# Attention on pairs of heads, with the softmax scale applied by the matrix product that transposes the probabilities

## The chip, the cores and the metric

The kernel runs on one core of one Trainium2 chip. The metric is the device time of one launch in microseconds (us), lower is better. The engines are TensorE (PE; its weight loads are listed apart as PEld), VectorE (DVE), ScalarE (ACT), GpSimd (POOL) and SyncE (SP).

## What is computed

Two transformer-like blocks in float32 on 512 tokens of width 1024. The first (four mixers, gates and a feed-forward layer) is not touched. The second has two layers. In each, 12 heads of 64 columns attend among the tokens and 4 heads read 256 memory rows; a projection and a convolutional feed-forward layer follow.

```python
# layer 0: causal attention with a forget term
c = lax.cumsum(log_f, axis=2)                  # per head, log_f = log_sigmoid(...)
sc = einsum(q, k) * dh ** -0.5
sc = sc + ci[..., :, None] - c[..., None, :]
sc = where(kpos <= qpos, sc, NEG)
out = softmax(sc) @ v
# layer 1: q, k with rotary embedding; three dilated branches of the same
# scores, which the kernel joins to one softmax with an additive 512x512 mask
# both layers, memory heads, no mask
sc = einsum(qm, km) * HEAD_DIM ** -0.5
out = softmax(sc) @ vm
h = h + merge_heads(heads) @ w_out[layer]
```

The term `ci` is the same along a row of scores and drops out of the softmax, so the kernel adds only the part that depends on the key.

## The kernel before, in words

Weights stream in as 334 pieces of 128 x 1024. Each weight product is done as three products of fp32r operands (high x high, high x low, low x high; `product`, L1277): the activations stand split in `h_hi`/`h_lo` (for projections from x) and `g_hi`/`g_lo` (for projections from hidden values or heads). POOL issues the loads of the weights and makes their low parts (L320 to L328).

Five engines run programs of their own, in the order in which their code is written, and wait for each other by semaphores. There is no scheduler: a wait in an engine's code holds everything behind it on that engine. Around attention the stages of a layer are:

1. Projections from x: 6 tiles of q (128 columns, so two heads each), 6 of k, 6 of v, in layer 0 one for the forget gates, 2 for the queries of the memory heads. DVE takes them out of the PSUM banks. In layer 0 it writes q and k at L628, one instruction per head into rows 0 to 63 of the tiles `q` and `k` of the arena: a head has all its 64 columns on rows 0 to 63 and a 512-column stretch of its own. In layer 1 ACT copies first (L1192), PE makes the rotated copy (`swap`, L1315) and DVE adds up (L638 to L641). v is transposed by PE (`turn_values`, L1328) and put back by DVE (L650).
2. Before the first of these DVE sets row 64 of all of `q` to 1.0 (L622, a memset of 1 x 8192), in both layers. In layer 0 the running sum of the forget gates is copied by one SP DMA into row 64 of `k`, so that a score product over 65 rows adds the forget term.
3. Memory keys and values: four more tiles from `mn`, the normalised memory.
4. Attention (`attention` on PE and the loops over `UNITS` on DVE and ACT): 64 units per layer, one unit is a head and a block of 128 queries. A unit of a mixing head has 128, 256, 384 or 512 keys, of a memory head 256. Per unit:
   - PE: the scores into bank ps0 to ps3 in turn (L1345); in layer 0 a second product adds the causal mask to the last 128 columns: identity x mask, both f32 (L1348).
   - DVE: in layer 1 the mask is added (L697); then the row maximum (L699).
   - ACT: exponential with the row sum (L1217) into one of 4 buffers `probs`.
   - DVE: reciprocal (L705), the whole row of probabilities times it (L706).
   - PE: one transpose per 128 keys into bank ps4 or ps5 (L1375), which ACT copies to `pt` (L1225).
   - After the first unit of the next head PE multiplies the values by `pt` (L1361, 4 products of 512, 384, 256 and 128 columns) into rows 0 to 63 or 64 to 127 of bank ps6 or ps7; ACT and DVE split the result into `g_hi` and `g_lo` (L1209, L686, 64 rows each).

   PE's loop writes the scores of unit u+2 ahead of the transposes of unit u:

```python
for u, (head, qb, width, _) in enumerate(UNITS):
    if u + 2 < len(UNITS):
        scores(u + 2)                       # from u = 4 waits for exped of u-4
    pe.wait_ge(S("probs"), before + u + 1)
    if u >= 2:
        pe.wait_ge(S("probs_kept"), before + u - 1)
    ...                                     # transposes of unit u
    if qb == 0 and head:
        head_output(head - 1)
```

   ACT's loop does the exponential of unit s, then the copy of unit s-2. DVE's loop does the maximum of unit s, then the scaling of unit s-1.
5. Projection of the heads into x (8 tiles) and the feed-forward layer.

The mask of layer 0 (640 KB, `mask_fox`) is loaded by SP into `work` after the forget row has landed. That of layer 1 is loaded in the same way after its rotary step.

## Time and profile before

| what | value |
| --- | --- |
| runs | 2654.08 us median of 3 (2653.63 to 2654.12) |
| profiled execution | 2655.1 us, span 2653.3 us |
| mean granted TensorE clock | 0.915 |
| PE busy | 2316.0 us, 87% of the span |
| DVE, ACT, POOL busy | 1475.5, 450.8, 845.2 us (56%, 17%, 32%) |
| chain that ended last, by engine | PE 71%, DVE 19%, DMA 5%, ACT 2%, issue 2% |
| attention of layer 0 | 1292.0 to 1434.9 us of the span |
| attention of layer 1 | 2022.0 to 2209.0 us of the span |

How to read it. Times count from the start of the span. An engine is busy while an instruction of it runs; matmuls are pipelined, so the duration listed for one holds its passage through the array too, and the step from the start of one to the start of the next tells what it costs in a row of them. A row of the timeline joins like instructions: `x8` is eight matmul records, and a product of f32 operands has two records (two passes) where a transpose or a product of fp32r operands has one. `[0.44 <-ACT arena L1225]` is idle time of the engine ahead of the row, and what ended it. The granted clock is 1.00 at 2.4 GHz and 0.50 at 1.2 GHz; between two such levels a mean over a stretch tells how it was divided. Row labels in the trace name the tile written and the tiles read.

### The profile page before, as it was taken

To read this page: it belongs to the slowest core of one execution; us is meant where nothing else is said; L and a number is where in the kernel's file an instruction comes from. 1 tells how busy PE (TensorE), PEld (TensorE's weight loads), DVE (VectorE), ACT (ScalarE), POOL (GpSimd) and SP (SyncE) were. 2 spreads that over 40 slices of the span, in tenths; PEclk is the share of its full clock that TensorE was granted. 3 is DMA by queue.
4 is the path that set the end of the run, shared out by engine and by line. 5 is a ranking of instruction groups with operands and counts; after the bars stand their busy time and mean duration, and the time that the engine had idled before them with its cause. 6 is when DMAs were issued, how large, how long until landed. Compare 5 with 4: busy or idle time off the path is not lost.

```text
span 2653.3 us, 26772 instructions
## 1 busy us (share of the span) xinstructions
PE 2316.0 (87%) x10172; PEld 1774.1 (67%) x10172; DVE 1475.5 (56%) x2162; ACT 450.8 (17%) x887; POOL 845.2 (32%) x1006
## 2 busy tenths in 40 slices
PE   1967999669669999989888999998988889999995
PEld 1745677557548888868655878787765336878784
DVE  6368866744674422574454654636654554736464
ACT  1010002111000000210354211112102442201011
POOL 1312333101224444434201444444332003444442
PEclk9978999756879999999899999999997678999998
DMA  7635687312869999968503889898774006889895
GB/s 238 145 70 110 125 166 161 76 30 51 261 188 230 193 195 193 193 147 182 114 1 80 190 180 193 174 194 187 167 154 101 1 1 128 190 184 193 179 195 130
DMA packets 114935, 390.73 MB, mean 147 GB/s; under 512 B 20460, under 2 KB 20972, under 8 KB 114296
## 3 DMA queue, kind: packets, MB, share of 16 engines
q0 software_dynamic: 96192, 350.27, 62.0%
q1 hardware_dynamic: 18616, 38.76, 4.2%
q8 instruction: 81, 1.33, 0.2%
q14 instruction: 46, 0.38, 0.1%
HBM read 386.33 MB, written 2.62 MB: 147 GB/s over the span
## 4 chain that ended last, share of the span: by engine, by line
PE 71%; DVE 19%; DMA 5%; issue 2%; ACT 2%; POOL 0%; SPq 0%; DVEq 0%; ACTq 0%
PE ps L1277 57%; PE ps L1361 4%; DMA arena<-in_ada 3%; PE ps L1345 2%; DMA w_lo<-in_w 2%; DVE small L699 1%; DVE arena L437 1%; PE ps L1375 1%; DVE work L706 1%; PE ps L1497 1%; DVE work L542 1%; DVE h_lo L354 1%; DVE g_lo L686 1%; DVE arena L725 1%; DVE g_lo L354 1%
## 5 line engine op out<-in xcount | busy, mean ns | idle before, releaser
L1277 PE MATMUL ps<-h_hi,w_hi 128*128 128x512 f32 x1760 | 713.2, 405 | 50.2 <-DVE h_lo L354 28.3
L320 POOL DMA_DIRECT2D w_hi<-in_w x334 | 186.1, 557 | 1623.6 <-PE ps L1277 1622.7
L1277 PE MATMUL ps<-h_lo,w_hi 128*128 128x512 f32 x1760 | 695.0, 395 | 0.0
L1277 PE MATMUL ps<-h_hi,w_lo 128*128 128x512 f32 x1760 | 694.2, 394 | 0.0
L1277 PEld LDWEIGHTS ps<-h_hi,w_hi 128*128 128x128 f32 x1760 | 336.7, 191 | 143.0 <-issue 36.1
L1277 PE MATMUL ps<-g_hi,w_hi 128*128 128x512 f32 (+1 forms) x880 | 346.6, 394 | 54.5 <-DVE g_lo L354 21.2
L1277 PEld LDWEIGHTS ps<-h_lo,w_hi 128*128 128x128 f32 x1760 | 337.2, 192 | 74.0 <-issue 6.7
L1277 PEld LDWEIGHTS ps<-h_hi,w_lo 128*128 128x128 f32 x1760 | 336.4, 191 | 71.9
L325 POOL TENSOR_SCALAR w_lo<-w_hi 128x1024 fp32r<-128x1024 f32 x334 | 359.5, 1076 | 36.5 <-DMA w_hi<-in_w 30.7
L1277 PE MATMUL ps<-g_lo,w_hi 128*128 128x512 f32 (+1 forms) x880 | 341.6, 388 | 0.0
L1277 PE MATMUL ps<-g_hi,w_lo 128*128 128x512 f32 (+1 forms) x880 | 341.3, 388 | 0.0
L328 POOL DMA_DIRECT2D w_lo<-in_w x334 | 300.3, 899 | 116.3 <-POOL w_lo L325 116.3
L1277 PEld LDWEIGHTS ps<-g_hi,w_hi 128*128 128x128 f32 x880 | 169.6, 193 | 99.4 <-DVE g_lo L354 23.7
L1277 PEld LDWEIGHTS ps<-g_lo,w_hi 128*128 128x128 f32 x880 | 170.2, 193 | 32.6 <-issue 0.7
L1277 PEld LDWEIGHTS ps<-g_hi,w_lo 128*128 128x128 f32 x880 | 169.5, 193 | 33.6
L1243 ACT ACTIVATE arena<-arena,vec 128x512 f32<-128x512 f32 x88 | 71.8, 816 | 416.4 <-DVE arena L720 408.9
L731 DVE TENSOR_TENSOR x<-ps,x 128x512 f32<-128x512 f32 x48 | 33.2, 692 | 186.5 <-PE ps L1277 186.5
L720 DVE TENSOR_TENSOR arena<-ps,work 128x512 f32<-128x512 f32 x88 | 60.8, 691 | 98.8 <-PE ps L1277 97.3
L1345 PE MATMUL ps<-arena 64*128 64x256 f32 (+7 forms) x256 | 113.7, 531 | 1.2 <-DVE work L677 1.2
L725 DVE SCALAR_TENSOR_TENSOR arena<-arena,vec 128x511 f32<-128x511 f32 x88 | 111.7, 1270 | 3.6 <-ACT arena L1243 0.6
L952 DVE TENSOR_TENSOR arena<-arena 128x512 f32<-128x512 f32 x32 | 53.0, 1657 | 76.9 <-ACT arena L1170 76.9
L353 DVE CAST g_hi<-arena 128x512 fp32r<-128x512 f32 (+1 forms) x100 | 82.8, 828 | 6.3 <-ACT arena L1104 2.9
(335 smaller groups left out, 2246.3 us busy)
## 6 DMA issues: line engine op xcount, KB each, us to landing
w_hi<-in_w POOLq DMA_DIRECT2D x334, 512.0 KB, 3.8
w_lo<-in_w POOLq DMA_DIRECT2D x334, 512.0 KB, 5.6
arena<-in_ada SPq DMA_DIRECT2D x48, 512.0 KB, 8.4
x<-in_xT SPq DMA_DIRECT2D x1, 2048.0 KB, 16.2
x<-in_xT SPq DMA_DIRECT2D x4, 512.0 KB, 4.9
arena<-in_memT SPq DMA_DIRECT2D x2, 1024.0 KB, 5.1
out_y<-arena SPq DMA_DIRECT2D x1, 2048.0 KB, 6.3
work<-in_mask_fox SPq DMA_DIRECT2D x1, 640.0 KB, 7.0
```

The source lines that it names most:

```text
L320: pool.dma_start(w_hi[:, q % SLOTS, :], A["w"][q]).then_inc(S(f"high_in{q % SLOTS}"), 16)
L325: pool.tensor_scalar(w_lo[:, q % SLOTS, :], w_hi[:, q % SLOTS, :].bitcast(F32), -1.0, 0.0, ALU.mult, ALU.add).then_inc(S("negated"), 1)
L328: pool.dma_start(w_lo[:, q % SLOTS, :], A["w"][q], accum_op=ALU.add).then_inc(S(f"low_in{q % SLOTS}"), 16)
L353: do(dve.tensor_copy(hi, src))
L354: do(dve.tensor_tensor(lo, src, hi.bitcast(F32), ALU.subtract), name)
L720: do(dve.tensor_tensor(cv_m["z"][:, side, :], tile()[:], rstd, ALU.mult), "conv_scaled")
L725: do(dve.scalar_tensor_tensor(dst[:, 1:], z[:, :T - 1], w(1), dst[:, 1:], ALU.mult, ALU.add))
L952: do(dve.tensor_tensor(s, r, r, ALU.mult), "relu_used")
L1243: do(act.activation(c[:, j % 2, :], cv_m["z"][:, side, :], ACT.Identity, scale=V("cw2", at), bias=V("cb2", 44 * layer + 22 * side + j0 + j ...
L1277: mm = pe.matmul(bank, w[:, slot, cols], a(k), start=(k == 0 and i == 0), stop=(k == blocks - 1 and i == 2))
L1345: mm = pe.matmul(ps[u % BANKS][:, 0:width], at_m["q"][0:rows, head, P * qb:P * qb + P], keys, start=True, stop=not masked)
L1361: mm = pe.matmul(ps[6 + head % 2][out_rows, q0:T], values, at_m["pt"][:, b, q0:T], start=(b == 0), stop=(b == blocks - 1))
```

## The change

It groups the heads in pairs, 8 per layer (6 mixing, 2 memory), so that there are 32 units per layer in place of 64.

- Layout: `q`, `k` and `km` hold a pair in one 512-column stretch, the even head on rows 0 to 63, the odd one on 64 to 127. The evictions at L628, L641, L668 and L672 become one instruction of 128 rows each in place of two of 64. The ones row and its memset (L622) go.
- Scores: two products of 64 rows, one per head, into two neighbouring banks (L1362).
- Forget term, layer 0: the running sum is split into three fp32r parts (4 small DVE instructions), which 6 SP DMAs put on rows 0 to 2 and 64 to 66 of `h_lo`. For each head an fp32r product with ones in three of 64 rows (`parts_r`) adds it to all columns (L1366).
- Causal mask, layer 0: fp32r product of `eye_r` and `causal_r` (L1368), both 128 x 128. With `parts_r` they are loaded at the program's start by three POOL DMAs, which stand ahead of the first `load_low`. The 640 KB load of `mask_fox` is gone.
- Softmax: one DVE maximum for both heads (L706), in layer 1 one mask addition for both; two exponentials (L1233); one reciprocal of two columns (L712); DVE then writes for each head the 128 x 128 identity times the reciprocal (L716) and leaves the probabilities as they are.
- Transpose: a plain f32 product of each block of probabilities with that diagonal matrix (L1397).
- Outputs: for each key block one product per head, into rows 0 to 63 and 64 to 127 of one bank (L1381). The split into `g_hi` and `g_lo` is done once per pair, on 128 rows (L1221, L693).
- Buffers: 3 sets of probabilities of two heads in place of 4 of one; `pt` twice, each for two heads; banks ps4 and ps5 take head 0 and head 1 of every unit, so that PE waits for the copy of unit u-1 where it waited for that of unit u-2; scores wait for the exponentials of unit u-2 where they waited for u-4.

Its core as a diff:

```diff
-UNITS = [(h, b, (b + 1) * P, b * (b + 1) // 2 * P) for h in range(NH) for b in range(QB)] + \
-        [(NH + h, b, MT, 0) for h in range(NMH) for b in range(QB)]
+NP, NMP = NH // 2, NMH // 2
+UNITS = [(pair, b, (b + 1) * P, b * (b + 1) // 2 * P) for pair in range(NP) for b in range(QB)] + \
+        [(NP + pair, b, MT, 0) for pair in range(NMP) for b in range(QB)]
+P_SETS = 3
...
# SP, layer 0
-                    sp.dma_start(at_m["k"][HD:HD + 1, :, :], work[0:NH, 4, :]).then_inc(S("forget_in"), 16)
-                    sp.wait_ge(S("forget_in"), 16)
-                    sp.dma_start(masks, A["mask_fox"]).then_inc(S("mask_in"), 16)
+                    sp.wait_ge(S("forget_parts"), 1)
+                    sp.wait_ge(S("tile"), n_fox_done)
+                    for g in range(2):
+                        for part in range(3):
+                            sp.dma_start(h_lo[64 * g + part:64 * g + part + 1, 0:NP, :].bitcast(F32),
+                                         work[g:NH:2, part, :]).then_inc(S("forget_in"), 16)
...
# DVE
-                do(dve.memset(q[HD:HD + 1, :, :], 1.0))
-                            bank = tile()
-                            for g in range(2):
-                                do(dve.scalar_tensor_tensor(dst[0:HD, 2 * i + g, :], bank[64 * g:64 * g + 64, :],
...
+                            do(dve.scalar_tensor_tensor(dst[:, i, :], tile()[:], HD ** -0.5 if name == "q" else 1.0, rstd,
+                                                        ALU.mult, ALU.mult), "dve_freed")
...
-                        do(dve.tensor_reduce(top, src, AX.X, ALU.max, negate=True), "score_top")
+                        src, top = banks8[:, 2 * (s % 2):2 * (s % 2) + 2, 0:width], small[:, 33 + s % P_SETS, 0:2]
+                        do(dve.tensor_reduce(top, src, AX.X, ALU.max, negate=True), "score_top")
...
-                        do(dve.reciprocal(rec, small[:, 33 + u % 4, 2:3]))
-                        do(dve.tensor_scalar(pr, pr, rec, None, ALU.mult), "probs")
+                        do(dve.reciprocal(row[:, 2:4], row[:, 4:6]))
+                        if u >= 2:
+                            dve.wait_ge(S("probs_turned"), 2 * (before + u - 1))
+                        for g in range(2):
+                            do(dve.tensor_scalar(at_m["scale"][:, u % 2, g, :], K("ident"), row[:, 2 + g:3 + g], None, ALU.mult), "probs")
...
# ACT
+                        if s >= P_SETS:
+                            act.wait_ge(S("probs_turned"), 2 * (before + s - P_SETS + 1))
+                        for g in range(2):
...
+                            do(act.activation(pr, src, ACT.Exp, bias=row[:, g:g + 1], accum_out=row[:, 4 + g:5 + g]),
+                               "exped" if g else "act_step")
+                        for g in range(2):
+                            need("probs_turned")
+                            do(act.activation(pt[pair % 2][:, g, 0:blocks, P * qb:P * qb + P],
+                                              ps[4 + g][:, 0:width].rearrange("p (a b) -> p a b", a=blocks), ACT.Copy), "probs_kept")
...
# PE
-                    if u >= BANKS:
-                        pe.wait_ge(S("exped"), before + u - BANKS + 1)
+                    if u >= 2:
+                        pe.wait_ge(S("exped"), before + u - 1)
+                    for g in range(2):
+                        keys = at_m["k"][half(g), pair, 0:width] if pair < NP else at_m["km"][half(g), pair - NP, :]
+                        mm = pe.matmul(bank(g)[:, 0:width], at_m["q"][half(g), pair, P * qb:P * qb + P], keys,
+                                       start=True, stop=not fox)
+                    if fox:
+                        for g in range(2):
+                            pe.matmul(bank(g)[:, 0:width], parts_r[half(g), :], h_lo[half(g), pair, 0:width], start=False, stop=False)
+                        for g in range(2):
+                            mm = pe.matmul(bank(g)[:, P * qb:P * qb + P], eye_r[:], causal_r[:], start=False, stop=True)
...
-                    if u >= 2:
-                        pe.wait_ge(S("probs_kept"), before + u - 1)
-                    for b in range(width // P):
-                        mm = pe.transpose(ps[4 + u % 2][:, P * b:P * b + P], probs[u % 4][:, P * b:P * b + P], K("ident"))
+                    for g in range(2):
+                        pe.wait_ge(S("probs"), 2 * (before + u) + g + 1)
+                        if u:
+                            pe.wait_ge(S("probs_kept"), 2 * (before + u - 1) + g + 1)
+                        for b in range(width // P):
+                            mm = pe.matmul(ps[4 + g][:, P * b:P * b + P], probs[u % P_SETS][:, g, P * b:P * b + P],
+                                           at_m["scale"][:, u % 2, g, :], start=True, stop=True)
```

What it moves, first on TensorE in layer 0, from the outputs of one head (before) or pair (after) to the transposes of the third unit behind it. In these rows `64x512` is the shape written, `arena` holds q, k, the values, `pt` and some of the probabilities, `work` the other probabilities and the mask, `con` the identity. Before:

```order
L1361 MATMUL ps<-arena 64x512
L1361 MATMUL ps<-arena 64x384
L1361 MATMUL ps<-arena 64x256
L1361 MATMUL ps<-arena 64x128
L1345 MATMUL ps<-arena 128x512
L1348 MATMUL ps<-work,con 128x128
L1375 MATMUL ps<-con,arena 128x128 x2
L1345 MATMUL ps<-arena 128x128
L1348 MATMUL ps<-work,con 128x128
L1375 MATMUL ps<-con,work 128x128 x3
```

After:

```order
L1381 MATMUL ps<-arena 64x512 x2
L1381 MATMUL ps<-arena 64x384 x2
L1381 MATMUL ps<-arena 64x256 x2
L1381 MATMUL ps<-arena 64x128 x2
L1362 MATMUL ps<-arena 128x512 x2
L1366 MATMUL ps<-h_lo,parts_r 128x512 x2
L1368 MATMUL ps<-causal_r,eye_r 128x128 x2
L1397 MATMUL ps<-arena,work 128x128 x4
L1362 MATMUL ps<-arena 128x128 x2
L1366 MATMUL ps<-h_lo,parts_r 128x128 x2
L1368 MATMUL ps<-causal_r,eye_r 128x128 x2
L1397 MATMUL ps<-arena 128x128 x6
```

The order of the steps is kept, each step now serves two heads, and the forget product is new. On ScalarE, at the same place, before (one head):

```order
L1225 ACTIVATE arena<-ps 128x128
L1209 ACTIVATE g_hi<-ps 64x512
L1217 ACTIVATE work,small<-ps,small 128x512
L1225 ACTIVATE arena<-ps 128x2x128
L1217 ACTIVATE arena,small<-ps,small 128x128
```

and after (one pair):

```order
L1241 ACTIVATE arena<-ps 128x128 x2
L1221 ACTIVATE g_hi<-ps 128x512
L1233 ACTIVATE arena,small<-ps,small 128x512 x2
L1241 ACTIVATE arena<-ps 128x2x128 x2
L1233 ACTIVATE arena,small<-ps,small 128x128 x2
```

Both exponentials of the widest unit (L1233, 128x512) now stand ahead of the two copies of the unit with 256 keys (L1241, 128x2x128), on which TensorE's next turns depend.

## Rows read from the trace of the kernel before

**Rows 1.** The chain that ended last, of the page, by line.
```profile
PE ps L1277 57%; PE ps L1361 4%; DMA arena<-in_ada 3%; PE ps L1345 2%; DMA w_lo<-in_w 2%; DVE small L699 1%; DVE arena L437 1%; PE ps L1375 1%; DVE work L706 1%; PE ps L1497 1%; DVE work L542 1%; DVE h_lo L354 1%; DVE g_lo L686 1%; DVE arena L725 1%; DVE g_lo L354 1%
```

**Rows 2.** Busy times of the two attention stages: start:end, us, PE, PEld, DVE, ACT, POOL, PEclk.
```profile
1292.00:1434.90 142.90, 118.90 (x489) 67.39 (x489) 76.06 (x208) 76.65 (x209) 0.00 (x0) 0.94 0.03 6
2022.00:2209.00 187.00, 159.04 (x392) 65.11 (x392) 99.42 (x256) 78.36 (x209) 0.00 (x0) 0.69 0.01 3
```

**Rows 3.** TensorE in order of time, layer 0, one head: start, us, line, out<-in, shapes, passes.
```profile
1351.04 1.13 PE L1345 MATMUL ps<-arena 65*128 65x512 f32 x2
1352.01 0.39 PE L1348 MATMUL ps<-work,con 128*128 128x128 f32 x2
1352.23 0.38 PE L1375 MATMUL ps<-con,arena 128*128 128x128 f32 x2
...
1354.31 0.60 PE L1345 MATMUL ps<-arena 65*128 65x256 f32 x2
1354.75 0.39 PE L1348 MATMUL ps<-work,con 128*128 128x128 f32 x2
1354.97 0.66 PE L1375 MATMUL ps<-con,work 128*128 128x128 f32 x4
1355.46 0.81 PE L1345 MATMUL ps<-arena 65*128 65x384 f32 x2
...
1357.44 2.37 PE L1361 MATMUL ps<-arena 128*64 128x512 f32 x8 [0.44 <-ACT arena L1225]
1359.74 1.12 PE L1345 MATMUL ps<-arena 65*128 65x512 f32 x2
```

**Rows 4.** The same view, layer 0, heads that read the memory.
```profile
1403.34 0.70 PE L1345 MATMUL ps<-arena 64*128 64x256 f32 x2
...
1405.61 0.70 PE L1345 MATMUL ps<-arena 64*128 64x256 f32 x2
1406.29 0.44 PE L1375 MATMUL ps<-con,work 128*128 128x128 f32 x2
1406.66 0.70 PE L1345 MATMUL ps<-arena 64*128 64x256 f32 x2
...
1410.41 0.70 PE L1345 MATMUL ps<-arena 64*128 64x256 f32 x2
```

**Rows 5.** The same view, a product whose operands are fp32r.
```profile
1436.34 0.39 PE L1277 MATMUL ps<-g_hi,w_hi 128*128 128x512 f32 x1
1436.57 0.39 PE L1277 MATMUL ps<-g_lo,w_hi 128*128 128x512 f32 x1
```

**Rows 6.** The same view, two places with narrow tiles in the first block.
```profile
413.52 1.99 PE L1472 MATMUL ps<-arena,work 32*128 32x512 f32 x8
...
496.25 3.66 PE L1497 MATMUL ps<-con,arena 128*64 128x128 f32 x64
```

**Rows 7.** DVE and ACT in order of time, in the head of rows 3.
```profile
1352.53 0.69 DVE L699 TENSOR_REDUCE small<-ps 128x1 f32<-128x512 f32 x1 [3.42 <-PE ps L1348]
...
1355.68 0.42 DVE L699 TENSOR_REDUCE small<-ps 128x1 f32<-128x256 f32 x1
...
1353.31 0.69 ACT L1217 ACTIVATE work<-ps,small 128x512 f32<-128x512 f32 x1 [1.21 <-DVE small L699]
...
1354.12 0.38 ACT L1225 ACTIVATE arena<-ps 128x256 f32<-128x256 f32 x1
```

**Rows 8.** TensorE's waits before layer 0's attention.
```profile
PE ps L1277 <- DVE arena L628: 10.1, 1, 10.1
```

**Rows 9.** DVE in order of time, start of layer 0.
```profile
1165.16 6.88 DVE L622 MEMSET arena<- 1x8192 f32 x1 [1.76 <-issue]
```

**Rows 10.** TensorE's waits before layer 1's attention.
```profile
PE ps L1328 <- DVE arena L650: 7.7, 2, 7.3
PE ps L1315 <- ACT arena L1192: 4.2, 1, 4.2
```

**Rows 11.** DMA issues, of the page.
```profile
work<-in_mask_fox SPq DMA_DIRECT2D x1, 640.0 KB, 7.0
```

More of the change, by code:

```diff
@@ L1206, in _, with pair_high @@
                     values(6 + i, MT, layer)
-                def head_high(head):
-                    rows = slice(64 * (head % 2), 64 * (head % 2) + 64)
-                    do(act.activation(g_hi[rows, head // 2, :], ps[6 + head % 2][rows, :], ACT.Copy), "head_hi")
+                before = len(UNITS) * layer
+                def pair_high(pair):
+                    need("head_out")
+                    do(act.activation(g_hi[:, pair, :], ps[6 + pair % 2][:], ACT.Copy), "head_hi")
                 for s in range(len(UNITS) + 2):
@@ L1212, in _ @@
                     if s < len(UNITS):
[L1213 to L1214 removed]
+                        pair, qb, width, at = UNITS[s]
+                        row = small[:, 33 + s % P_SETS, :]
                         need("score_top")
[L1216 to L1217 removed]
+                        if s >= P_SETS:
+                            act.wait_ge(S("probs_turned"), 2 * (before + s - P_SETS + 1))
@@ L1221, in _ @@
[L1221 to L1223 removed]
+                        pair, qb, width, at = UNITS[u]
                         blocks = width // P
[L1225 to L1228 removed]
@@ L1381, in _ @@
+                    if qb == 0 and pair:
+                        pair_output(pair - 1)
+                pair_output(NP + NMP - 1)
             pe.wait_ge(S("con_in"), 16)
```

169 lines of the change are left out of this document (79 added, 90 removed).

## The prediction

> **What bounds the kernel now.** The chain of waits comes first: 57% of it is the weight products of L1277 [rows 1], which the change leaves alone. The lines it does touch (L1345, L1361, L1375, L699, L706, L686) each hold 1 to 4%, so the room lies in two short stages, and the next view is the table of those [rows 2]: attention of layer 0 takes 142.9 us, of layer 1 187.0. TensorE is busy for 83% and 85% of them, DVE and ACT for about half. So TensorE's own work is the first limit, waits the second. The granted clock is a third: 0.94 in layer 0 and 0.69 in layer 1. Between the two levels, 1.2 and 2.4 GHz, a mean of 0.69 is 62% of the time at the lower one.
>
> The timeline of one head at the full clock gives the prices [rows 3]. Steps between starts count, since listed durations overlap. A f32 product has two passes: 0.22 us for 128 columns (1352.01 to 1352.23), 0.44 for 256 (1354.31 to 1354.75), so 0.11 per pass and 128 columns, 0.65 for 384, 0.87 for 512. The row of 512 took 0.97: 0.1 more, behind outputs of another tile shape. Four transposes took 0.49: one pass each, 0.11 to 0.12. The outputs of a head took 2.30 (20 passes of 128 columns are 2.2), with 0.44 of waiting ahead. The head as a whole took 8.70 (1351.04 to 1359.74).
>
> **The steps of the change.**
>
> *Tile shape.* The heads that read memory have no mask product between scores and transposes, so products over 64 rows and over 128 rows alternate [rows 4]. There 256 columns of scores take 0.68 in place of 0.44 and two transposes 0.37 in place of 0.22: 0.39 per unit for the two changes of shape. I charge it to every unit after the change, since the 64-row products stand beside 128-row ones in all.
>
> *Side by side.* Can two products on different halves of the array run at once? Nothing in attention shows it, but the first block does [rows 6]: eight passes of 512 columns with 32-row tiles took 1.99 us, alone they would take 8 x 0.44 = 3.5; and 64 passes of 128 columns with 64-column tiles took 3.66, alone 64 x 0.11 = 7.0. The second is a full doubling. I take two tiles of 64 as fully overlapped: the scores of a pair cost what those of a head cost, and so do outputs.
>
> *Layer 0, a pair of mixing heads, TensorE's work.* Scores of 10 blocks: 10 x 0.22 + 0.1 = 2.3. Forget product, fp32r: a product of 512 columns steps by 0.23 [rows 5], so 0.23 + 0.17 + 0.12 + 0.07 = 0.6, both halves together. Causal products: 8 of 0.07 = 0.55 (in place of 8 f32 ones of 0.22). Turns: 20 blocks x 0.22 = 4.4; a plain f32 product has the two passes of L1348's, where the transpose had one, so this costs 2.2 more per pair than before. Outputs 2.3. Shape changes 4 x 0.39 = 1.6. Sum 11.7 us.
>
> *Its waits.* One is new. ACT's copy of the unit with 256 keys now stands behind both exponentials of the widest unit, and those behind a maximum over two heads. From that unit's scores: 0.1, the maximum (512 columns take 0.69, 256 take 0.42, so 1024 take 1.2 [rows 7]), 0.1, two exponentials with their row sums at 0.81 each (1353.31 to 1354.12), the copy 0.38, 0.1: 3.5 us. In that time TensorE has the turns of a unit (0.9) and the next scores (0.8). It waits about 1.75 per pair, and 0.35 in small pieces: 2.1. The pair takes 13.8, where two heads took 17.4.
>
> *Layer 0, the sum.* Memory heads took 7.07 each [rows 4]. A pair: 4 x (0.44 + 0.39) + 4 x 4 x 0.22 for turns + 4 passes of 0.44 for outputs: 8.6, with nothing for waits. I take 8.6 for the whole, since the wait of 1.8 hides part of the charge for shapes; without that it is 10.4, which goes into the range. What is left of the stage before, 142.9 - 12 x 8.70 - 4 x 7.07 = 10.2, is filling, draining and stretches at the low clock, and I keep it. After: 6 x 13.8 + 2 x 8.6 + 10.2 = 110.2, **32.7 less**.
>
> *Layer 1.* At the full clock TensorE's work per pair is 2.3 + 4.4 + 2.3 + 1.6 = 10.5. Its waits are longer: the mask addition over both heads, priced as the maximum (1.2), lies between scores and maximum. From the scores to the copy it is then 4.7 with 1.7 to hide it, and the narrow units too have a chain that is longer than the work beside it; I take 4.5, so 15.0. At the low clock the work doubles to 21 and hides most of the waits, 1.7 left: 22.7. Which clock? Before, TensorE's work here was scores and outputs on half of the array and single-pass transposes, and the clock was low for 62% of the time; layer 0, with mask products over all rows besides, held 0.94. After the change both halves work in scores and outputs, and the turns are two full passes. That speaks for the behaviour of layer 0, the longer waits against it. I take the low level for a fifth of the time: 16.5. Then 6 x 16.5 + 17.2 + 10.2 = 126.4, **60.6 less**. At 0.94 as in layer 0 it would be some 4 less, all low 37 more.
>
> *Before the stages.* TensorE waited 10.1 us for an eviction at L628 [rows 8]. DVE was late because of the memset on one partition, 6.88 and 1.76 idle ahead of it [rows 9]. Those go, and half of the first pair of evictions (0.7): **9.4 less**. What is late next is the normalising of the memory, which has 10 tiles of room. In layer 1 the same memset held the rotary steps: the wait of 4.2 goes, 1.2 at the clock behind it, and 1.6 of the 7.3 at L1328 [rows 10] since each L641 is one instruction: **7.0 less**. Bounds for both together: 9 (DVE finds another reason to be late) and 21.6 (all three waits gone).
>
> *DMAs and small instructions.* The mask load of 640 KB, 7.0 us to landing [rows 11], competed with weights: taken at **1.0 less**, between 0 and 3.4. The 6 forget DMAs and the 4 more DVE instructions have four memory tiles on TensorE to hide them, 96 products of 256 columns, by rows 5 some 11 us; without that cover they would cost at most 4 x 0.69 for DVE (no instruction on 512 columns in rows 7 is longer) and 7.0 for landing, as the far larger mask load. On SP nothing waits behind them but the mask, which has gone. The three POOL DMAs at the start of the program go out ahead of the first low part, which must wait for its weight piece to land anyway: 0, at most the 7.0 of the mask load, ten times the size of each. DVE's scaling shrinks from two rows of up to 512 to two of 128 columns; it is off the path except in the chain of a narrow unit.
>
> **Sum.** -32.7 - 60.6 - 9.4 - 7.0 - 1.0 = -110.7. Against the profiled execution: 2655.1 - 110.7 = 2544.4; the median of the runs is 1.0 lower than that execution, so **2543.5 us**.
>
> One rule speaks against the turns. First the row: L1348's f32 product took 0.22 where a transpose took 0.11 to 0.12 [rows 3], and that is what the sum uses. The Trainium skill, "TensorE: Matmul & The Clock Gate", section Terms, says of the transpose mode that it is four times faster for FP32. By that rule, as an estimate, a plain product would take four transposes, 0.44, which is case F below. The trace has the rule against it, with two.
>
> **The rivals.**
>
> *A. As summed*, 0.67: 2543.5. For it: the prices are of the same shapes at the same clock, and DVE and ACT, half idle, get less to do.
>
> *B. The 64-row tiles run one after another*, 0.10. Rows 6 show overlap with 32-row and with 64-column tiles, not with 64-row ones. Then scores cost 2.3 more per mixing pair, the forget product 0.6 more in layer 0, a memory pair 4 x 0.44 = 1.8 more: 6 x 2.9 + 6 x 2.3 + 4 x 1.8 = 38. Time 2582.
>
> *C. The clock of layer 1 stays low throughout*, 0.10. 22.7 per pair in place of 16.5 is +37, its two memory pairs +8: 2588.
>
> *D. Fewer waits and the full clock*, 0.05. The maximum of two banks is cheaper than summed, or the wait of 1.75 hides behind the shape changes. Layer 0 loses 9, layer 1 the 9 of the clock and 3 of waits: 2522.
>
> *E. Slower: the tiles do not overlap, in scores nor outputs, and with them half of the array idles, so the clock falls in both stages as it did in layer 1.* Chance 0.03. At the full clock a pair then takes 13.8 + 2.3 + 0.6 + 2.3 = 19 in layer 0 and 15.0 + 4.6 = 19.6 in layer 1, a memory pair 12.1: stages of 148 and 152, 300 in all, of which some 53 are waits (6 x 2.1, 6 x 4.5 and 13 of the 20 at the ends). At 0.69 [rows 2] the other 247 take 358: 411 against 330 before. Less 17 for the memsets and the mask load that is +64: 2719. The point from which it decides: 247/c + 53 = 347 gives a granted clock of 0.84. Above that it is still no loss. Against it: rows 6.
>
> *F. The turns cost four transposes*, 0.05. 152 blocks a layer, 304 in all, at 0.22 more: +67, so 2610. Against it stands the row of L1348; for it only that no row shows an f32 product whose stationary operand is the data and changes with each block. The page named above would make it so.
>
> **How the numbers follow.** The range is to hold 8 in 10. A itself runs from about 2522 to 2570: 10 either way for the waits and the shape changes (0.39 on 64 units is 25, and the memory pairs may cost 7 more), 10 for the clock of layer 1, 4 for the start of the stages. B and C lie at 2582 and 2588; E and F are left out. So **2514 to 2596**. A measurement of this kernel can tell about 0.2% (5 us) from no change. Of the cases only E is slower, and nothing lies near 2654 unless two of B, C and F meet: faster 0.96, same 0.01, slower 0.03.
>
> **What would show it.** The stages last about 110 and 126 us, a mixing pair 13.8 and 15 to 17 us from one 512-column L1362 to the next. The two L1362 of a unit start within 0.1 us of each other and the pair steps by one product's time (if 1.9 us for 512 columns, B). A turn L1397 steps by 0.22 (if 0.44, F). TensorE waits 1.6 to 1.8 us per mixing pair of layer 0 for the copy L1241 (if none, D). The granted clock in layer 1's stage is 0.85 or more (if 0.6, C; if both stages fall, E). The memset L622 and the wait of 10.1 are gone, and no other instruction of DVE holds the products of L1277 longer than 1 us there. The prediction is wrong if the stages shrink and the time doesn't follow, that is, if the products behind attention wait for weights; I charge nothing for that, since the chain has the loads of `w_lo` at 2% [rows 1].

## The result and the profile after

The changed kernel takes 2555.57 us (median of 4 runs, 2555.28 to 2556.54). The kernel before took 2653.86 in the same series (4 runs, 2645.27 to 2654.12). The ratio is 0.9638, with a 95% interval of 0.9618 to 0.9657: faster, by 98 us. The profiled execution has a span of 2553.8 us, 1.8 less than that median.

The two attention stages first, with the columns of [rows 2]:

```profile
1282.10:1398.10 116.00, 98.02 (x640) 67.69 (x640) 54.51 (x136) 71.85 (x201) 0.00 (x0) 0.94 0.03 6
1976.70:2108.10 131.40, 103.77 (x544) 70.29 (x544) 74.20 (x160) 73.60 (x201) 0.00 (x0) 0.79 0.03 7
```

To be read against [rows 2]: layer 0 went from 142.9 to 116.0 us at the same clock, 0.94. Layer 1 went from 187.0 to 131.4 and its clock from 0.69 to 0.79. DVE's busy time fell by a quarter in both, ACT's little. In order of the program, each stage taken from its first score product to the first weight product behind it:

| stretch | before, us | after, us | difference | predicted |
| --- | --- | --- | --- | --- |
| up to layer 0's attention | 1292.0 | 1282.1 | -9.9 | -10.4 |
| attention, layer 0 | 142.9 | 116.0 | -26.9 | -32.7 |
| up to layer 1's attention | 587.2 | 578.6 | -8.6 | -7.0 |
| attention, layer 1 | 187.0 | 131.4 | -55.6 | -60.6 |
| the rest | 444.3 | 445.7 | +1.4 | 0 |

The chain that ended last:

```profile
PE ps L1292 61%; PE ps L1397 3%; DMA arena<-in_ada 3%; PE ps L1362 2%; PE ps L1381 1%; DMA w_lo<-in_w 1%; DVE arena L450 1%; DVE small L706 1%; PE ps L1520 1%; DVE work L555 1%; DVE h_lo L367 1%; DVE arena L735 1%; PE ps L1479 1%; DVE work L374 1%; DMA w_hi<-in_w 1%
```

The weight products (L1292 now) rose from 57% [rows 1] to 61% because the rest became shorter. The lines of attention are the turns L1397 (3%), the scores L1362 (2%) and the outputs L1381 (1%).

TensorE in order of time, one mixing pair of layer 0, which answers to [rows 3]:

```profile
1347.30 1.13 PE L1362 MATMUL ps<-arena 64*128 64x512 f32 x4
1347.86 0.80 PE L1366 MATMUL ps<-h_lo,parts_r 64*128 64x512 f32 x2
1348.58 0.44 PE L1368 MATMUL ps<-causal_r,eye_r 128*128 128x128 f32 x2
1348.86 1.11 PE L1397 MATMUL ps<-arena,work 128*128 128x128 f32 x8
1349.89 0.49 PE L1362 MATMUL ps<-arena 64*128 64x128 f32 x4
...
1352.59 1.58 PE L1397 MATMUL ps<-arena 128*128 128x128 f32 x12 [1.77 <-ACT arena L1241]
1354.09 0.70 PE L1362 MATMUL ps<-arena 64*128 64x256 f32 x4
...
1355.12 2.00 PE L1397 MATMUL ps<-arena 128*128 128x128 f32 x16
1357.05 0.92 PE L1362 MATMUL ps<-arena 64*128 64x384 f32 x4
...
1361.42 1.13 PE L1362 MATMUL ps<-arena 64*128 64x512 f32 x4
```

Scores of both heads for 512 keys (L1362, four passes) step by 0.56 us to the forget product, and forget and causal products by another 1.0. A single 512-column f32 product took 0.97 in rows 3 before the change. So two 64-row products do run at once. In layer 1, below, where nothing stands between scores and turns, the two take 1.05 for the pair. The pair as a whole takes 14.12 us (1347.30 to 1361.42), where two heads took 17.4. Its one long wait is 1.77 us for the copy L1241. DVE and ACT at that place:

```profile
1349.13 1.22 DVE L706 TENSOR_REDUCE small<-ps 128x2 f32<-128x1024 f32 x1 [2.85 <-PE ps L1368]
...
1350.44 0.69 ACT L1233 ACTIVATE arena<-ps,small 128x512 f32<-128x512 f32 x1 [2.29 <-DVE small L706]
...
1351.25 0.69 ACT L1233 ACTIVATE arena<-ps,small 128x512 f32<-128x512 f32 x1
...
1352.06 0.80 ACT L1241 ACTIVATE arena<-ps 128x256 f32<-128x256 f32 x2
```

One sees the chain that the prediction wrote down: the maximum of 1024 columns 1.22, both exponentials with their row sums from 1350.44 to 1352.02, and the copy only then. ACT had idled 2.29 us just before, while the turns that it was to copy were done by 1349.9.

The same in layer 1:

```profile
2018.36 1.13 PE L1362 MATMUL ps<-arena 64*128 64x512 f32 x4
2019.41 1.16 PE L1397 MATMUL ps<-arena 128*128 128x128 f32 x8
2020.50 0.49 PE L1362 MATMUL ps<-arena 64*128 64x128 f32 x4
2024.37 2.90 PE L1397 MATMUL ps<-arena 128*128 128x128 f32 x12 [3.38 <-ACT arena L1241]
2027.20 1.23 PE L1362 MATMUL ps<-arena 64*128 64x256 f32 x4
2028.36 2.98 PE L1397 MATMUL ps<-arena,work 128*128 128x128 f32 x16
...
2035.36 1.13 PE L1362 MATMUL ps<-arena 64*128 64x512 f32 x4
```

The pair takes 17.0 us. The mask addition makes the wait 3.38 us. Behind it twelve passes of turns take 2.83 us, where they took 1.50 in layer 0: the granted clock is 0.50 (1.2 GHz) there, and it comes back during the sixteen passes that follow. A pair of memory heads, in the same view:

```profile
2086.39 0.70 PE L1362 MATMUL ps<-arena 64*128 64x256 f32 x4
...
2089.71 1.13 PE L1397 MATMUL ps<-arena,work 128*128 128x128 f32 x8 [0.89 <-ACT arena L1241]
...
2091.73 1.13 PE L1397 MATMUL ps<-arena 128*128 128x128 f32 x8 [0.26 <-ACT arena L1241]
...
2094.08 1.13 PE L1397 MATMUL ps<-arena 128*128 128x128 f32 x8 [0.59 <-ACT arena L1241]
2095.14 1.94 PE L1381 MATMUL ps<-arena,work 128*64 128x512 f32 x8
2097.01 0.70 PE L1362 MATMUL ps<-arena 64*128 64x256 f32 x4
```

That is 10.6 us (2086.39 to 2097.01), of which 1.74 are three waits for the copy L1241. TensorE's waits ahead of the two stages, which answer to [rows 8, 10]:

```profile
PE ps L1292 <- DVE arena L637: 0.8, 1, 0.8
...
PE ps L1343 <- DVE arena L655: 6.3, 2, 5.5
```

The 10.1 us of [rows 8] are 0.8, and the memset is gone. The wait for ACT at the rotary step is gone too, and the 7.3 us for the values have become 5.5.

### The profile page after: what moved, and what is told of

It reads as the page before. It is cut to its first block, busy times and chain, and to the rows that moved or that the text cites. A ratio compares the mean times of both kernels' runs of the same rounds, so it can differ in the third digit from the quotient of the medians.

```text
span 2553.8 us, 27023 instructions
## 1 busy us (share of the span) xinstructions
PE 2241.6 (88%) x10476; PEld 1780.8 (70%) x10476; DVE 1410.6 (55%) x1964; ACT 441.1 (17%) x871; POOL 847.9 (33%) x1009
## 4 chain that ended last, share of the span: by engine, by line
PE 74%; DVE 16%; DMA 5%; ACT 2%; issue 2%; SPq 0%; POOL 0%; DVEq 0%; ACTq 0%
PE ps L1292 61%; PE ps L1397 3%; DMA arena<-in_ada 3%; PE ps L1362 2%; PE ps L1381 1%; DMA w_lo<-in_w 1%; DVE arena L450 1%; DVE small L706 1%; PE ps L1520 1%; DVE work L555 1%; DVE h_lo L367 1%; DVE arena L735 1%; PE ps L1479 1%; DVE work L374 1%; DMA w_hi<-in_w 1%
## 5 line engine op out<-in xcount | busy, mean ns | idle before, releaser
L1292 PE MATMUL ps<-h_hi,w_hi 128*128 128x512 f32 x1760 | 713.9, 406 | 40.2 <-DVE h_lo L367 27.9
L1292 PE MATMUL ps<-h_lo,w_hi 128*128 128x512 f32 x1760 | 696.0, 395 | 0.0
L1292 PE MATMUL ps<-h_hi,w_lo 128*128 128x512 f32 x1760 | 695.0, 395 | 0.0
L1292 PEld LDWEIGHTS ps<-h_hi,w_hi 128*128 128x128 f32 x1760 | 337.0, 191 | 133.9 <-DVE h_lo L367 28.3
L1292 PE MATMUL ps<-g_hi,w_hi 128*128 128x512 f32 (+1 forms) x880 | 346.6, 394 | 53.9 <-DVE g_lo L367 21.7
L1292 PEld LDWEIGHTS ps<-h_lo,w_hi 128*128 128x128 f32 x1760 | 337.2, 192 | 74.6 <-issue 6.9
L1292 PEld LDWEIGHTS ps<-h_hi,w_lo 128*128 128x128 f32 x1760 | 337.0, 191 | 71.8
L1292 PE MATMUL ps<-g_lo,w_hi 128*128 128x512 f32 (+1 forms) x880 | 342.2, 389 | 0.0
L1292 PE MATMUL ps<-g_hi,w_lo 128*128 128x512 f32 (+1 forms) x880 | 341.9, 389 | 0.0
L1292 PEld LDWEIGHTS ps<-g_hi,w_hi 128*128 128x128 f32 x880 | 169.8, 193 | 97.4 <-DVE g_lo L367 24.3
L1292 PEld LDWEIGHTS ps<-g_lo,w_hi 128*128 128x128 f32 x880 | 169.9, 193 | 33.2 <-issue 0.7
L1292 PEld LDWEIGHTS ps<-g_hi,w_lo 128*128 128x128 f32 x880 | 169.7, 193 | 33.5
L1397 PE MATMUL ps<-arena 128*128 128x128 f32 x416 | 71.1, 326 | 27.0 <-ACT arena L1241 26.8
L1397 PEld LDWEIGHTS ps<-arena 128*128 128x128 f32 x416 | 62.1, 230 | 42.1 <-issue 35.4
## 6 DMA issues: line engine op xcount, KB each, us to landing
x<-in_xT SPq DMA_DIRECT2D x1, 2048.0 KB, 17.4
```

What stands on the lines that cost most here:

```text
L1292: mm = pe.matmul(bank, w[:, slot, cols], a(k), start=(k == 0 and i == 0), stop=(k == blocks - 1 and i == 2))
L1397: mm = pe.matmul(ps[4 + g][:, P * b:P * b + P], probs[u % P_SETS][:, g, P * b:P * b + P], at_m["scale"][:, u % 2, g, :], start=True, stop= ...
```

## The experiments

The theory after this reading: the change is worth what the prediction's sum says, minus a new wait which the order of ScalarE's program makes, and in layer 1 that wait also costs clock. The rivals: the wait is one for DVE in truth and would only change its name; the turns as products are what costs; the clock of layer 1 is low for the narrow products, whatever the wait. The kernel before took 2649.2 to 2651.2 us (medians) in the series below, with single runs from 2640.6 to 2661.3. So differences between experiments are read by their ratios to it, and by the stages in their traces. Each stage here is taken as in the table above:

| kernel | time, us | ratio to before (95%) | layer 0, us, clock | layer 1, us, clock |
| --- | --- | --- | --- | --- |
| before | 2653.9 | 1 | 142.9, 0.94 | 187.0, 0.69 |
| the change | 2555.6 | 0.9638 (0.9618 to 0.9657) | 116.0, 0.94 | 131.4, 0.79 |
| e1_copy_first | 2514.5 | 0.9487 (0.9469 to 0.9505) | 99.7, 0.97 | 103.2, 0.93 |
| e2_transposes | 2543.7 | 0.9601 (0.9581 to 0.9621) | 116.9, 0.80 | 120.1, 0.79 |
| e3_both | 2504.4 | 0.9442 (0.9424 to 0.9460) | 93.0, 0.95 | 102.6, 0.83 |
| e4_outputs_apart | 2577.2 | 0.9720 (0.9702 to 0.9738) | 127.2, 0.92 | 137.9, 0.86 |
| e5_memset_back | 2576.6 | 0.9715 (0.9693 to 0.9737) | 115.0, 0.96 | 131.2, 0.80 |
| e6_wait_filled | 2542.9 | 0.9598 (0.9573 to 0.9622) | 114.0, 0.96 | 118.8, 0.97 |
| e7_scale_first_transposes | 2556.1 | 0.9642 (0.9606 to 0.9678) | 112.3, 0.85 | 134.2, 0.69 |
| e8_scale_first | 2547.5 | 0.9608 (0.9565 to 0.9652) | 107.1, 0.95 | 128.1, 0.88 |
| e9_before_copy_first | 2641.7 | 0.9962 (0.9943 to 0.9982) | 132.4, 0.97 | 178.0, 0.74 |
| e10_before_filled | 2626.8 | 0.9912 (0.9886 to 0.9937) | 139.2, 0.96 | 160.4, 0.93 |
| e11_both_filled | 2502.9 | 0.9451 (0.9434 to 0.9469) | 93.5, 0.95 | 99.1, 0.98 |
| e12_copy_first_filled | 2509.4 | 0.9472 (0.9454 to 0.9490) | 99.7, 0.97 | 100.2, 0.97 |

### The copies ahead of the exponentials

```diff
                 for s in range(len(UNITS) + 2):
+                    if s >= 2:
+                        u = s - 2
...
+                            do(act.activation(pt[pair % 2][:, g, 0:blocks, P * qb:P * qb + P],
+                                              ps[4 + g][:, 0:width].rearrange("p (a b) -> p a b", a=blocks), ACT.Copy), "probs_kept")
                     if s < len(UNITS):
...
                             do(act.activation(pr, src, ACT.Exp, bias=row[:, g:g + 1], accum_out=row[:, 4 + g:5 + g]),
                                "exped" if g else "act_step")
-                    if s >= 2:
-                        u = s - 2
...
-                        if qb == 0 and pair:
-                            pair_high(pair - 1)
+                    if s >= 2 and UNITS[s - 2][1] == 0 and UNITS[s - 2][0]:
+                        pair_high(UNITS[s - 2][0] - 1)
```

> ScalarE does the copies of unit s-2 ahead of the exponentials of unit s. If TensorE's waits for the copy (14.1 us in layer 0's attention, 22.2 in layer 1's) come from the order of ScalarE's program, they go: ScalarE is idle for 2.3 us at that place in layer 0, waiting for the maximum. A pair then takes 12.3 to 12.6 us in place of 14.1 in layer 0, and in layer 1 some 12.5 to 14 in place of 17.0, since the clock stays up too: 2515 to 2530 in all. Rival: the wait only changes its name (for the exponentials, or for DVE's diagonals) with the same length: 2550 to 2556.

Measured: 2514.5 us, 41 less than the change. In the trace layer 0's pairs from the second on take 12.31 us, at the short end of what was expected. Layer 1, TensorE in order of time:

```profile
2000.01 1.60 PE L1397 MATMUL ps<-arena 128*128 128x128 f32 x12 [1.65 <-DVE arena L716]
2001.54 0.70 PE L1362 MATMUL ps<-arena 64*128 64x256 f32 x4
2002.17 2.05 PE L1397 MATMUL ps<-arena,work 128*128 128x128 f32 x16
...
2012.44 1.95 PE L1397 MATMUL ps<-arena,work 128*128 128x128 f32 x12 [1.65 <-DVE arena L716]
2014.32 1.23 PE L1362 MATMUL ps<-arena 64*128 64x256 f32 x4
2015.47 2.75 PE L1397 MATMUL ps<-arena 128*128 128x128 f32 x16
...
2021.94 0.70 PE L1362 MATMUL ps<-arena 64*128 64x512 f32 x2
```

The wait for the copy is gone. What is left is 1.65 us for a diagonal (L716), which on DVE stands behind the mask addition and the maximum of the widest unit. The two pairs shown have the same wait of 1.65, and behind the first the clock held (12 passes in 1.53, the pair 12.4), behind the second it fell (1.88 for the 12, then a low clock in the scores and 16 passes that follow, the pair 13.8). The stage:

```profile
1963.60:2066.80 103.20, 86.94 (x544) 56.49 (x544) 74.18 (x160) 73.66 (x201) 0.00 (x0) 0.93 0.04 8
```

So the first rival falls: a wait with another name did stay in layer 1, at half its length, but none of that size in layer 0. And with no product added and the wait halved, layer 1's clock rose from 0.79 to 0.93.

### The scaling back on DVE, the transposes back on TensorE

```diff
-                            do(dve.tensor_scalar(at_m["scale"][:, u % 2, g, :], K("ident"), row[:, 2 + g:3 + g], None, ALU.mult), "probs")
+                            pr = probs[u % P_SETS][:, g, 0:width]
+                            do(dve.tensor_scalar(pr, pr, row[:, 2 + g:3 + g], None, ALU.mult), "probs")
...
-                            mm = pe.matmul(ps[4 + g][:, P * b:P * b + P], probs[u % P_SETS][:, g, P * b:P * b + P],
-                                           at_m["scale"][:, u % 2, g, :], start=True, stop=True)
+                            mm = pe.transpose(ps[4 + g][:, P * b:P * b + P], probs[u % P_SETS][:, g, P * b:P * b + P], K("ident"))
```

> The change with its scaling undone: DVE scales the whole rows again, TensorE transposes with one pass per block. If the product costs two passes where the transpose has one, TensorE's work falls by 2.2 us per mixing pair and 1.8 per memory pair; part of it turns into longer waits for the copy (0.4 per pair), so layer 0's stage gets about 12 us shorter, and layer 1's about the same if its clock holds: 2530 to 2545. Rival: DVE's scaling of 512 columns (0.49 against 0.30 us for a diagonal) and the emptier array take it back, the granted clock of layer 1 falls from 0.79 towards 0.69: 2555 to 2575.

Measured: 2543.7, 12 less than the change, as the theory had it in sum and not in its parts. The stages:

```profile
1284.50:1401.40 116.90, 94.83 (x489) 54.41 (x489) 60.36 (x136) 71.98 (x201) 0.00 (x0) 0.80 0.03 6
1974.70:2094.80 120.10, 83.47 (x393) 43.27 (x393) 80.04 (x160) 73.70 (x201) 0.00 (x0) 0.79 0.03 6
```

Layer 0 gained nothing (116.9 against 116.0): its pairs take 13.7 in place of 14.1, with a wait for the copy of 2.25 in place of 1.77, and now the clock fell in each of them, so that the stage has 0.80 against 0.94. Layer 1 gained 11.3 at the same 0.79. Pairing alone, without the product that scales, is thus no worse than the change as made.

> Both edits: copies first, and transposes with rows scaled by DVE. If waits and passes are independent terms, the gains of the two add up, 2500 to 2515. Rival: with one pass per block there is too little work on TensorE to cover the chain of maximum, exponential and scaling, so it is no faster than the copies first alone, and the clock falls.

Both edits of the two experiments above together. Measured: 2504.4, ratio 0.9442. That is 51 us below the change, and the best version of the study together with e11. The stages, then the eight transposes of the unit with 512 keys in layer 0 and the wait that is left in layer 1:

```profile
1283.50:1376.50 93.00, 80.20 (x488) 44.74 (x488) 60.32 (x136) 71.97 (x201) 0.00 (x0) 0.95 0.04 8
1954.30:2056.90 102.60, 79.45 (x393) 40.55 (x393) 80.04 (x160) 73.69 (x201) 0.00 (x0) 0.83 0.04 6
```

```profile
1329.26 1.06 PE L1396 MATMUL ps<-con,arena 128*128 128x128 f32 x8
1330.27 0.92 PE L1361 MATMUL ps<-arena 64*128 64x384 f32 x4
...
1990.99 1.54 PE L1396 MATMUL ps<-con,arena 128*128 128x128 f32 x6 [2.28 <-DVE arena L715]
```

Eight transposes step by 1.01 us to the next scores, where the change's sixteen passes step by 1.93 (1355.12 to 1357.05). Once the copy no longer holds TensorE, that difference reaches the time: layer 0 is at 93.0 against e1's 99.7. In layer 1 the two are even (102.6 and 103.2), since TensorE waits 2.28 us per pair here, for the rows of 384 columns, which DVE scales behind the mask addition and the maximum of the widest unit.

### The wait filled

In layer 1, per mixing pair, 14 products of identity by identity into the idle output bank, ahead of the turns of the unit with 256 keys. The result is not used. They stand one group of turns ahead of the place where the wait was, and what follows moves back by their time.

```diff
+                    if layer == 1 and qb == 1 and pair < NP:
...
+                        for i in range(14):
+                            pe.matmul(ps[6 + pair % 2][:, P * (i % 4):P * (i % 4) + P], K("ident"), K("ident"), start=True, stop=True)
```

> In layer 1 TensorE does 14 products of identity by identity (3.1 us at the full clock) in the 3.4 us in which it waits for the copy; their result is not used. If the low clock behind that wait (12 turns in 2.8 us in place of 1.5, 16 in 2.9 in place of 1.9) comes from the wait alone, a pair falls from 17.0 to about 14.2 us, the granted clock of the stage from 0.79 to over 0.95, the time to about 2539. Rival: the clock is low for the mix of narrow products in the stage, whatever the wait: the time stays at 2555 or grows.

Measured: 2542.9, a pair 15.18 us in place of 17.0, the stage 118.8 in place of 131.4. One of these places and the stage:

```profile
1997.47 3.39 PE L1396 MATMUL ps<-con 128*128 128x128 f32 x28
2000.69 1.06 PE L1402 MATMUL ps<-arena,work 128*128 128x128 f32 x8
```

```profile
1973.60:2092.40 118.80, 103.95 (x712) 73.34 (x712) 74.18 (x160) 73.67 (x201) 0.00 (x0) 0.97 0.03 7
```

The clock is 0.97, with the same narrow products and the unused ones beside them. So the narrow products by themselves do not hold the clock down. This run alone can't tell the wait that is gone from the full products that came in; that the wait counts is shown by the copies moved ahead, where nothing was added. The low level cost 1.8 us per pair, where I had written 2.8 ahead of the run. The remainder are short waits of 0.2 to 0.5 for copies, 1.2 in all, which now stand elsewhere.

The same was done to the kernel before, 6 products in the wait of 1.47 us that each of its heads has in layer 1:

> The kernel before, with 6 products of identity by identity (1.3 us) in layer 1 in the wait of 1.5 us that each head has. Their result is not used. If the low clock of that stage (0.69) comes from such waits with light products around them, the clock rises to over 0.9 and the stage falls from 187 to 145 to 155 us: 2615 to 2625. Then some 30 of the 56 us that the change gains in layer 1 are the clock. Rival: the clock stays near 0.7, the stage at 185 to 200.

Measured: the stage 160.4 us against 187.0, most heads 10.0 each.

```profile
2058.96 1.60 PE L1375 MATMUL ps<-con 128*128 128x128 f32 x12
```

```profile
2020.30:2180.70 160.40, 137.63 (x537) 69.37 (x537) 99.41 (x256) 78.36 (x209) 0.00 (x0) 0.93 0.02 5
```

So filling the waits, with all the work of before left in, gives 26.6 of the 55.6 us that the change gained in layer 1; the stage's share went from 62% of the time at 1.2 GHz to 15%. The time was 2626.8 and the stage 160.4, both above what I expected, and the ratio 0.9912.

> As e3_both, with 10 unused products of identity by identity (2.2 us) per mixing pair in layer 1, in TensorE's wait of 2.3 us ahead of the transposes of the unit with 384 keys. If that wait is what takes the clock down to 0.83 there, a pair falls from 12.6 to about 11.3 us and the time from 2504 to 2495 to 2498. Rival: one-pass transposes keep the array too empty, the clock stays below 0.9 and nothing is gained: 2502 to 2508.

Measured: a clock of 0.98 in the stage, which became 3.5 us shorter (99.1 against 102.6), and 2502.9 us: by their intervals the runs do not tell it from e3. The clock did what I expected and the time did not, so neither the expectation nor its rival holds whole. The mixing pairs stayed at 12.6, not 11.3, because a second wait came up in each; what the stage gained lies in its first units and the memory pairs:

```profile
2005.79 0.65 PE L1401 MATMUL ps<-con,arena 128*128 128x128 f32 x2 [1.19 <-DVE arena L715]
```

It is for the scaling of the unit with 128 keys, and is 0.47 in e3: the low clock had covered the rest.

> As e1_copy_first, with 7 such products (1.5 us) in its wait of 1.65 us per pair in layer 1. There the pairs take 12.2 us where the clock holds and 13.8 where it falls: with the wait filled all take 12.2, the stage 98 to 99 in place of 103.2, 2509 to 2511 in all. Rival: no change, 2512 to 2516. Against e11 it tells what the diagonal product still costs when neither version loses by the clock: 10 to 15 us, layer 0's part of it 7.

Measured: 2509.4 as expected, layer 1 at 100.2 us with 12.2 to 12.4 per pair, the stage 1 us longer than I had it. Against e11, with both at full clock, the diagonal product costs 6.2 us in layer 0 and 1.1 in layer 1: 7 in all, where I expected 10 to 15. In layer 1 it is nearly free: the mixing pairs are even shorter with it (12.2 against 12.6, DVE having less to scale ahead of the turns), the memory pairs longer.

### DVE scales first

On DVE, reciprocal and scaling of unit s-1 were moved ahead of the mask addition and maximum of unit s, on top of e3 with its transposes (e7) and on top of e1 with the diagonal (e8).

> Copies first and transposes as in e3_both, and DVE scales unit s-1 ahead of the mask addition and maximum of unit s. In e3_both TensorE still waits 2.3 us per pair in layer 1 (0.7 in layer 0) for a scaling that stands behind the addition and the maximum of the widest unit. If that order is the wait, it goes, and the clock of layer 1 rises from 0.83: layer 1 about 11.5 us per pair in place of 12.6, layer 0 10.3 in place of 11.0: some 2492 in all. Rival: DVE itself is full in layer 1 (about 11.2 us of work per pair with rows scaled), and a later maximum delays the exponentials as much: 2500 to 2508.

> As e1_copy_first (copies first, scale in the product), with the same new order on DVE. The wait of 1.65 us per pair for a diagonal in layer 1 goes and the clock stays up: 11.5 per pair in place of 12.2 to 13.8, layer 0 unchanged at 12.3: 2503 to 2508. If DVE's load decides in layer 1, this version with the lighter DVE work has the shorter layer 1 of the two. Rival: unchanged, 2512 to 2516.

Measured: 2556.1 and 2547.5 us, 52 and 33 slower than e3 and e1. This was a clear miss. DVE in order of time in layer 0 of e8, then TensorE:

```profile
1311.38 0.17 DVE L701 RECIPROCAL small<-small 128x2 f32<-128x2 f32 x1 [1.56 <-ACT arena L1241]
1311.59 0.61 DVE L705 TENSOR_SCALAR arena<-con,small 128x128 f32<-128x128 f32 x2
1312.23 1.22 DVE L716 TENSOR_REDUCE small<-ps 128x2 f32<-128x1024 f32 x1
...
1315.18 0.70 PE L1362 MATMUL ps<-arena 64*128 64x256 f32 x4 [0.69 <-ACT arena L1241]
```

DVE now waits for the exponentials of unit s-1 (L1241 here, 1.56 us) before it starts the maximum of unit s, at 1312.23. ScalarE waits for that, and TensorE waits for the exponentials, because only two pairs of score banks are there (0.69 us at 1315.18). Maximum, exponential and scaling of successive units stand in one line where they overlapped before. In layer 1 these waits reach 3 us, and with transposes (e7) the clock is down to 0.69 there.

### Parts of the sum

The outputs, head after head in place of side by side:

```diff
-                    for b in range(blocks):
-                        q0 = P * b if pair < NP else 0
-                        for g in range(2):
+                    for g in range(2):
+                        for b in range(blocks):
+                            q0 = P * b if pair < NP else 0
```

> The products for the outputs of a pair in another order: all of head 0, then all of head 1, so that only one product at the border can overlap. If the two 64-column tiles run at once in the change, a mixing pair gets about 2.1 us longer and a memory pair 0.9: +29, 2584. Rival: the outputs overlap for another reason, or hide in a wait: within 5 us of 2555.

Measured: +22 us where I expected 29, of which 17.7 lie in the two stages. The outputs of a mixing pair in layer 0, and those of a memory pair:

```profile
1304.19 3.93 PE L1381 MATMUL ps<-arena 128*64 128x512 f32 x16
1308.05 1.13 PE L1362 MATMUL ps<-arena 64*128 64x512 f32 x4
...
1400.35 1.94 PE L1381 MATMUL ps<-arena,work 128*64 128x512 f32 x8
```

The mixing pair's take 3.86 (1304.19 to 1308.05) against 2.31, so side by side is worth 1.55 there, and in layer 0 some pairs lose 1.4 more by the clock. The memory pair's take 1.9, exactly as in the change (1.94 listed in both): the order did not matter there, see the last section. That is where the expectation was too high, with the 2.1 that it had for a mixing pair.

The memset, put back on a row that is written later anyway:

```diff
+                do(dve.memset(arena[HD:HD + 1, 0:8192 - T], 1.0))
```

> The change with a memset of one row (1 x 7680) put back ahead of the evictions of q, in both layers. If the 18 us gained ahead of the two attention stages came from the memset, +8 to +9 in layer 0 and +1 to +7 in layer 1: 2565 to 2572. Rival: they came from evictions with 128 rows in one instruction, and DVE has slack for the memset: under 2560.

Measured: +21 us, more than I expected. In the trace TensorE waits 8.9 us for the eviction again, and 3.4 at the rotary step. The stretch up to layer 0's attention is 13.6 us longer and the one up to layer 1's 7.4, while starts of that first stage differ by 7 us between kernels that are alike up to there: 1281.5 to 1288.5, mean 1284.3, in the change and nine of its variants, 1292.0 to 1297.3, mean 1295.4, in the kernel before and its two. By these means the change gained 11.1 us ahead of the first stage, and the memset takes back 11.4. So its price is about what the change gained there; little is left for the evictions of 128 rows.

### The same order of ScalarE in the kernel before

> The kernel before, with ScalarE's copies ahead of the exponentials except in the unit that must wait for the head's output. If the wait for the copy came in with the pairs, this gains little, at most 5 us, since TensorE waits there for DVE's scaling (17 us in layer 0), not for the copy: 2645 to 2654. Rival: the order of ScalarE's program costs as much before: 2610 to 2635.

Measured: ratio 0.9962, about 10 us, twice the bound that I gave and far from the rival. The profiled execution, with a span of 2635.3, is one of the shorter ones: its layer 0 is 10 us shorter than before and its layer 1 is 9, more together than the medians show. In layer 0 TensorE's waits for the scaling stay as they were (17 us); the 5.2 us in which outputs waited for a copy are 0.5. The order of ScalarE's work cost something before as well, but the large wait for the copy is the change's.

## Why the prediction was right, and where it was off

The time was 2555.6, 12 us above the forecast of 2543.5 and inside its range of 2514 to 2596. The likeliest case held, and its direction, mechanism and places were those seen; that layer 1 came out within 5 us is in part luck, as told below. Case C, with the low clock throughout layer 1, is out by the granted clock of 0.79 there, and D by the wait of 1.77. Term by term:

- *Side by side.* Right. Scores of 512 columns for two heads take 1.05 where one took 0.97, outputs 2.31 for two where 2.30 for one. Rival B is out by that, E with it. e4 prices the outputs' half.
- *Turns.* Right. Twelve passes step by 1.50 us, 0.25 per product with the change of tile shape in it; rival F (0.44) is out. The Trainium skill's factor of four for FP32 in transpose mode ("TensorE: Matmul & The Clock Gate", section Terms) does not appear: sixteen passes of eight products took 1.93 us, eight transposes 1.01, a factor of 1.9.
- *The new wait of layer 0.* Right: 1.75 predicted, 1.77 measured, at the copy named. e1 showed it to be made by ScalarE's order. The prediction had the idle time of ScalarE in its reach and did not ask what the other order would give: 41 us.
- *A mixing pair of layer 0.* 13.8 predicted, 14.1 measured, +2.0 for six; one pair lost another 1.4 by the clock.
- *Memory pairs.* The step that failed most. It says that "8.6 for the whole" holds "since the wait of 1.8 hides part of the charge for shapes". They took 10.6, the other end that it kept for the range (10.4). The shape changes do not hide the wait: TensorE's own work there is 8.9 us, and beside it stand 0.89, 0.26 and 0.59 us of waiting, now for ScalarE's copy where a head before waited for DVE's scaling. +4.0 in each layer, of which 2 came back at the ends of the stage.
- *Layer 1.* Nearly right in sum, by two errors of opposite sign. The sum had 15.0 us for a pair at the full clock, 4.5 of them waits, 22.7 at the low one, and the low one for a fifth of the time: 16.5. Measured were 17.0, with one wait of 3.4. At the full clock the pair is 15.2 (e6, whose unused products and short waits make 4.4), so that part was right. The low level's share was mis-sized: the stage's clock of 0.79 is 42% of the time, and the test that the prediction named for it (0.85 or more) failed. Its price was too high: by the sum that share would have cost 3.2 us per pair, and it cost 1.8, since slower products hide the short waits. The prediction's argument, that fuller products hold the clock, gave too little to the wait between them: halving it (e1) brought the clock from 0.79 to 0.93.
- *Ahead of the stages.* -9.9 and -8.6 against -10.4 and -7.0. e5 confirms the memset as their cause. The mask load's share of 1.0 was never seen: waits for `w_lo` there are 2.8 to 4.6 us in the eleven kernels without it and 3.8 to 5.2 in the three with it. It was not tried by itself, and stays open.

The account closes: +5.8 and +5.0 in the stages, +0.5 and -1.6 ahead of them, +1.4 behind, and 1.0 since the median lies 1.8 above the span in place of 0.8, together 12.1. What lies outside the stages, 1.6 us at most, is within the 7 us by which starts differ between kernels that are alike, and gets no cause.

## What to carry to other kernels

When a change doubles what each step does, read for every engine the order of its steps again: a copy that cost some 10 us in all behind one exponential (e9) held TensorE for far longer once it stood behind two, and moving it into the time in which ScalarE waited anyway gave 41 us, almost half as much again as the change. A scale that moves from DVE into a TensorE product makes TensorE's work longer and DVE's shorter, so ask which of the two the next step waits for; here it cost 6 us in layer 0 and was about even in layer 1. And add to a wait of TensorE the price of the low clock that can follow it: 1.8 us per pair behind a wait of 3.4 in layer 1, and in the kernel before filling such waits gave back 26.6 of 187 us.

## What was not expected of the hardware

- *How far apart in program order two tiles still overlap.* In e4 all passes of head 0 precede those of head 1. In the single records of the mixing pair the first pass of head 1 starts at 1305.750, 0.006 us after the fifth of head 0's eight and ahead of its sixth (1305.960), so three passes ahead of its turn. (The records name no head; the one of 512 columns behind those of 256 can only be head 1's first.) In a memory pair head 0 has four passes in all, and the two heads overlap entirely (1.9 us for eight passes of 512 columns), whatever the order. So TensorE here took up a pass for the other half of the array while the fourth pass before it in the program was only starting.
- *The clock behind a wait.* It fell to 1.2 GHz at the end of the waits of 3.4 us (the change, layer 1) in every pair, and of the four waits of 1.77 in layer 0 it fell behind one. In e1's layer 1 the same wait of 1.65 us with the same work around it let it fall in some pairs and not in others. With single-pass transposes it fell behind 2.25 us in layer 0 (e2), and behind 1.47 in the kernel before. Among the mixing pairs it mostly came back 3 to 7 us later; at the start of layer 1's stage it stayed low for 17 us. Filling the wait with unused products kept it up in nearly all of them.
